# A two-layer transformer step on one core: cast order at the merge's first tile, and where the products by sevens begin in the second layer

## The reference

```
h   = rms_norm(x) * (1 + scale1) + shift1
z   = h @ w_in                       # inputs of three mixers, and three gates
g   = sigmoid(z_gate)                # (B, L, 3, 1024)
out = (g[0]*y_a + g[1]*y_b + g[2]*y_c) @ w_out
x   = x + gate1 * out
h2  = rms_norm(x) * (1 + scale2) + shift2
x   = x + gate2 * (square(relu(h2 @ w_ff1)) @ w_ff2)
```

## Time and profile before

| what | value |
|---|---|
| time, median of 3 runs (lowest to highest) | 2067.82 us (2067.37 to 2068.98) |
| the profiled execution: its own time, and its span | 2063.75 us, 2062.0 us |
| mean granted TensorE clock | 0.992 |
| busy: PE, DVE, ACT, POOL | 96%, 59%, 46%, 14% |
| the chain that ended last: PE, DVE, ACT | 82%, 11%, 3% |

### The profile page before, as it was taken

The page is one execution under the profiler, slowest core; times in us unless marked ns, Lnnn a source line. Parts: engine busy times, 40 slices in busy tenths (PEclk is TensorE's granted clock), DMA queues, the critical chain, the costliest instruction groups (busy, mean ns, idle before and its releaser), DMA issues.

```text
span 2062.0 us, 34108 instructions
## 1 busy us (share of the span) xinstructions
PE 1980.4 (96%) x13976; PEld 1810.8 (88%) x13976; DVE 1217.4 (59%) x2095; ACT 946.0 (46%) x1746; POOL 284.7 (14%) x229
## 2 busy tenths in 40 slices
PE   6999999999999999999999999999999899999997
PEld 3995688899888999999989866888999899999997
DVE  4245688756468273736553466877664764646464
ACT  5535544534366161625454355453442743535262
POOL 1000000222012130403100000003220312121210
PEclk9999999999999999999999999999999999999999
DMA  9210001343523324242432100113443121213221
GB/s 367 74 51 11 1 27 52 114 166 128 188 81 112 144 91 150 68 149 88 158 109 74 36 6 1 47 58 120 163 162 124 51 89 65 94 62 103 62 94 60
DMA packets 53035, 195.92 MB, mean 95 GB/s; under 512 B 6032, under 2 KB 8144, under 8 KB 52112
## 3 DMA queue, kind: packets, MB, share of 16 engines
q1 hardware_dynamic: 49408, 174.61, 25.2%
q0 software_dynamic: 3472, 19.14, 2.6%
HBM read 187.79 MB, written 5.93 MB: 94 GB/s over the span
## 4 chain that ended last, share of the span: by engine, by line
PE 82%; DVE 11%; ACT 3%; issue 2%; DMA 2%; SPq 0%; ACTq 0%; DVEq 0%
PE ps L742 36%; PE ps L894 23%; PE ps L809 2%; PE ps L914 2%; PE ps L1060 2%; PE ps L923 2%; DVE w_lo_parts L1687 2%; PE ps L760 2%; PE ps L1036 2%; PE ps L847 2%; PE ps L1090 2%; PE ps L1065 1%; ACT scratch L1508 1%; DVE scratch L2095 1%; DVE merged L1764 1%
## 5 line engine op out<-in xcount | busy, mean ns | idle before, releaser
L1687 DVE TENSOR_TENSOR w_lo_parts<-w_raw,w_hi_parts 128x512 fp32r<-128x512 f32 x548 | 403.9, 756 | 242.9 <-ACT w_hi_parts L1274 148.2
L1274 ACT CAST w_hi_parts<-w_raw 128x512 fp32r<-128x512 f32 x296 | 172.1, 619 | 457.5 <-PE ps L742 413.4
L742 PE MATMUL ps<-hid_hi_parts,w_hi_parts 128*128 128x320 f32 x1216 | 280.3, 312 | 2.3 <-DVE merged L2154 1.6
L742 PE MATMUL ps<-hid_lo_parts,w_hi_parts 128*128 128x320 f32 x1216 | 277.0, 309 | 0.0
L742 PE MATMUL ps<-hid_hi_parts,w_lo_parts 128*128 128x320 f32 x1216 | 276.9, 309 | 0.0
L1885 DVE SCALAR_TENSOR_TENSOR x<-ps,modulation,x 128x128 f32<-128x128 f32 (+2 forms) x216 | 81.7, 434 | 319.0 <-PE ps L742 319.0
L742 PEld LDWEIGHTS ps<-hid_hi_parts,w_hi_parts 128*128 128x128 f32 x1216 | 201.9, 188 | 25.3 <-issue 22.1
L1278 ACT CAST w_hi_parts<-w_raw 128x512 fp32r<-128x512 f32 x252 | 152.2, 621 | 137.5 <-PE ps L742 56.7
L742 PEld LDWEIGHTS ps<-hid_lo_parts,w_hi_parts 128*128 128x128 f32 x1216 | 203.3, 188 | 0.0
L742 PEld LDWEIGHTS ps<-hid_hi_parts,w_lo_parts 128*128 128x128 f32 x1216 | 203.3, 188 | 0.0
L894 PE MATMUL ps<-h_hi_parts,w_hi_parts 128*128 128x320 f32 x560 | 173.8, 310 | 0.0
(11 more groups left out here) (334 smaller groups left out, 4080.9 us busy)
## 6 DMA issues: line engine op xcount, KB each, us to landing
w_raw<-in_stream SPq DMA_DIRECT2D x312, 512.0 KB, 3.9
scratch<-in_first SPq DMA_DIRECT2D x10, 512.0 KB, 14.3
small_weights<-in_small POOLq DMA_DIRECT2D x2, 2048.0 KB, 10.5
h_scratch<-in_first SPq DMA_DIRECT2D x6, 512.0 KB, 17.3
x<-in_xT POOLq DMA_DIRECT2D x2, 1280.0 KB, 11.8
x<-in_xT POOLq DMA_DIRECT2D x8, 320.0 KB, 4.1
x_kept<-x POOLq DMA_DIRECT2D x8, 320.0 KB, 2.5
x<-x_kept POOLq DMA_DIRECT2D x8, 320.0 KB, 4.1
```

What stands on the lines that cost most here:

```text
L742: ins = mm(out[:, h, :], weight(w, s, k), a[:, k, h * HALF:(h + 1) * HALF], start=(first and n == 0), stop=(last and n == 2))
L1274: copy(place(wh, r), raw_half(s, n)).then_inc(w_hi, 1)
L1687: return tt(dst, full, hi.bitcast(F32), ALU.subtract)
```

## The change

Three edits. (1) At m = 0 of the mix, in both layers, ACT first waits for the gate product and casts the two weight halves, and only then does `first_gate(0)` (for q = 0) and the sigmoid out of PSUM; before, both sigmoids stood ahead of the casts. (2) Of the low parts at m = 0, DVE makes part 1 after b = 0, part 2 after b = 1 and part 3 after b = 2; before, parts 1 and 2 after b = 0, part 3 after b = 1. (3) In the second layer the first feed-forward block goes by sevens from tile 6 on: tiles 4 and 5 become whole products, and only the pair (6, 7) is by sevens. `first_seven(l, f)` says where it begins, and the counts of finished products (`done`) and the loops of PE, ACT and DVE follow it; ACT's two `cast_diff` stay at q = 2 and 3.

```
--- before.py
+++ after.py
@@ -118,6 +118,11 @@
 SEVEN = 7
 
 
+def first_seven(l, f):
+
+    return 0 if f > 0 else 4 if l == 0 else 6
+
+
 def by_sevens(s):
 
     i = s % PER
@@ -125,7 +130,7 @@
         m, q = divmod(i - MIX0, 3)
         return m >= 1 and q < 2
     f, q = divmod(i - FF0, 2 * KT)
-    return f >= 0 and q in (range(4, KT) if f == 0 else range(KT))
+    return f >= 0 and q in range(first_seven(s // PER, f), KT)
 
 
 def leads(s):
@@ -161,17 +166,17 @@
 PLAIN = [plain(s) for s in range(MAIN)]
 
 
-def whole_product(o):
+def whole_product(o, l):
 
     if O_MIX <= o < O_OUT:
         m, q = divmod(o - O_MIX, 5)
         return m == 0 or q >= 2
-    return o < O_FF or not by_sevens(FF0 + o - O_FF)
-
-
-def done(o):
-
-    return sum(whole_product(n) for n in range(o + 1)) + (KT if o >= O_MIX else 0)
+    return o < O_FF or not by_sevens(l * PER + FF0 + o - O_FF)
+
+
+def done(o, l=0):
+
+    return sum(whole_product(n, l) for n in range(o + 1)) + (KT if o >= O_MIX else 0)
 
 
 def blocks_until(s):
@@ -191,7 +196,7 @@
         m, q = divmod(i - MIX0, 3)
         n = done(O_MIX + 5 * m + (q if q < 2 else 3 + half))
     else:
-        n = done(O_OUT + (i - OUT0))
+        n = done(O_OUT + (i - OUT0), l)
     return l * DONE + n
 
 
@@ -1225,7 +1230,7 @@
                 last_two(0, O_OUT + OUT_TILES - 2, OUT0 + OUT_TILES - 2, hh, hl)
                 for f in range(FF_BLOCKS):
                     i, o = FF0 + 2 * KT * f, O_FF + 2 * KT * f
-                    for q in range(4 if f == 0 else 0):
+                    for q in range(first_seven(e.layer, f)):
                         if q == 0:
                             first_two(o, i, 1, True)
                         elif q > 1:
@@ -1233,9 +1238,9 @@
                             banks_read(o + q)
                             product(pair(o + q), i + q, hh, hl)
                         modulation(i + q)
-                    for q in range(4 if f == 0 else 0, KT, 2):
+                    for q in range(first_seven(e.layer, f), KT, 2):
                         n = o + q
-                        first = q == (4 if f == 0 else 0)
+                        first = q == (first_seven(e.layer, f))
                         pair_by_sevens(n, i + q, {0: n - 2, 2: n - 1} if first else {0: n - 4, 2: n - 2, 3: n - 1})
                     for q in range(KT if f < FF_BLOCKS - 1 else KT - 2):
                         tile_ready(i + KT + q)
@@ -1601,12 +1606,12 @@
 
                     if m == 0:
                         act.wait_ge(gate_sb, e.at(gate_sb, 2 * KT))
-                    if m == 0:
-                        first_gate(0)
                     for q in range(2 if m == 0 else 0):
                         act.wait_ge(mm_done, e.at(mm_done, done(o + q)))
+                        split_next(i + q)
+                        if q == 0:
+                            first_gate(0)
                         fn(halves(G[:, 1 + q, :]), pair(o + q), ACT.Sigmoid).then_inc(pair_free[(o + q) % 2], 1)
-                        split_next(i + q)
                         modulation(i + q)
                         for n in range(2 * q, 2 * q + 2):
                             cast_diff(True, n)
@@ -1640,13 +1645,14 @@
                     if f == 1:
                         act.preload_act_table_set(LN)
                     i, o = FF0 + 2 * KT * f, O_FF + 2 * KT * f
-                    for q in range(4 if f == 0 else 0):
-                        act.wait_ge(mm_done, e.at(mm_done, done(o + q)))
+                    for q in range(first_seven(e.layer, f)):
+                        act.wait_ge(mm_done, e.at(mm_done, done(o + q, e.layer)))
                         split_next(i + q)
                         fn(halves(gqk[:, q % 2, :]), pair(q), ACT.Relu).then_inc(pair_free[q % 2], 1)
-                        if q >= 2:
+                        if q in (2, 3):
                             cast_diff(False, 2 * q - 4)
                             cast_diff(False, 2 * q - 3)
+                        if q >= 2:
                             act.wait_ge(pair_free[q % 2], e.at(pair_free[q % 2], (o + q) // 2 + 1))
                             act.wait_ge(hid_ready, e.at(hid_ready, q - 1))
                             fn(hid[:, q % 2, :], gqk[:, q % 2, :], ACT.Square).then_inc(hid_sq, 1)
@@ -1658,8 +1664,8 @@
                         if q == 1:
                             full_h(1)
                         modulation(i + q)
-                    for q in range(4 if f == 0 else 0, KT, 2):
-                        pair_by_sevens(f, q, o, q == (4 if f == 0 else 0))
+                    for q in range(first_seven(e.layer, f), KT, 2):
+                        pair_by_sevens(f, q, o, q == (first_seven(e.layer, f)))
                         modulation(i + q)
                         modulation(i + q + 1)
                     hid_by_sevens(f, KT - 1, o)
@@ -1818,11 +1824,11 @@
                     if j == 0:
                         add_square(KT - 3)
                 half_sum(b, 0)
-                dve.wait_ge(mm_done, e.at(mm_done, done(o)))
+                dve.wait_ge(mm_done, e.at(mm_done, done(o, e.layer)))
                 add_half(KT - 2, o, gate, HALVES[1]).then_inc(pair_free[0], 1)
 
             def last_add(o, gate):
-                dve.wait_ge(mm_done, e.at(mm_done, done(o)))
+                dve.wait_ge(mm_done, e.at(mm_done, done(o, e.layer)))
                 add_half(KT - 1, o, gate, HALVES[1]).then_inc(pair_free[1], 1)
 
             def hat(n, p, k):
@@ -2160,7 +2166,7 @@
                         if b == 2:
                             tt(out, out, halves(tmp), ALU.add).then_inc(gate_scratch_free, 1)
                         if m == 0:
-                            for n in ((1, 2), (3,), ())[b]:
+                            for n in ((1,), (2,), (3,))[b]:
                                 low_diff(True, n)
                         if m == KT - 1:
                             for k in ((0, 1, 2), (3,), ())[b]:
@@ -2215,7 +2221,7 @@
                     for q in range(KT if f < FF_BLOCKS - 1 else KT - 2):
                         if f == 0 and q == 0:
                             dve.wait_ge(mod_read, 6 * e.layer + 6)
-                        dve.wait_ge(mm_done, e.at(mm_done, done(o + KT + q)))
+                        dve.wait_ge(mm_done, e.at(mm_done, done(o + KT + q, e.layer)))
                         add_to_x(q, q, 5).then_inc(pair_free[q % 2], 1)
                         if f == FF_BLOCKS - 1 and q >= 2:
                             add_square(q - 1)
```

6 lines of the change are left out of this document (3 added, 3 removed).

## The result

The changed kernel took 2053.32 us, median of 4 runs (2052.7 to 2056.31), against 2067.6 (2064.77 to 2068.98) for the kernel before: a ratio of 0.9933 with a 95% interval of 0.9917 to 0.9949. Timed again on another chip it took 2054.26 us (6 runs) against 2067.81 (14 runs), ratio 0.9932 (0.9918 to 0.9946). That is 14 us less, 11 to 17 by the interval.

The account below looks back on a forecast made before the run. PE, busy 96%, was taken as the bound, with DVE's queue setting its pace at the waits. Gains of 4.8 us in the mix and 4.2 in the feed-forward made 9.0 off 2067.82: 2058.8 us, range 2056.5 to 2063.4.

Parts of the forecast that it names:

- 10.5 us in 7 waits: PE's block products near the change: total time PE stood waiting for low weight halves from DVE.
- Edit 1, q = 0: Mix, both layers: casts fill ACT's wait before the sigmoids, so DVE's first low half starts 3.2 us earlier.
- Edit 1, q = 1: Mix: DVE waits 1.3 us for block 0's cast, keeping 1.9; PE loses 0.35 us per layer before b = 1.
- The same three operations in another order, so block 4's low half gains nothing: Mix, DVE: making low parts one by one brings block 4's low half no earlier, being behind all three.
- I take an unchanged toll: First layer's mix: POOL's four block sums still cost DVE some 3.5 us, as before the change.
- all four sums could block DVE: Mix: each POOL sum could cost DVE 1.1 us, 4.4 at most, making the total gain 7.2 instead of 9.0.
- Edit 3: Second layer's feed-forward: whole tiles 4 and 5 cost PE 1.76 us but remove waits, gaining 4.2 us (3.0 to 4.3).
- The same 9.0 off 2067.82: Whole kernel: the 9.0 us taken off the profiled span also comes off the runs' median, giving 2058.8 us.
- (a): Rival, mix: POOL eats DVE's head start or casts come late; only the order helps, 1.0 us; 2062.6 us, chance 0.13.
- (b): Rival, second layer's feed-forward: waits move to tile 6 and PE has 12 more matmuls; 2064.8 us, chance 0.08.
- (c): Rival, changed places: no effect, PE arrives earlier and waits for weights from memory; about 2067.5 us, chance 0.07.
- (d): Rival, mix at q = 1: sigmoid behind casts waits for a late raw tile; slower, 2072.8 us, chance 0.03.

Follow-up runs that it names:

- before_4: One traced execution of the unchanged kernel before, with clock falls in the second mix and second feed-forward; no total time given, 14 feed-forward blocks took 30.91 us.

## Why the prediction was wrong, point by point

- **PE's work and restarts:** right. 1.76 us for 12 matmuls, 0.1 for a restart.
- **"10.5 us in 7 waits" near the change:** misread in part. Three of the seven, 2.2 us, were in the first layer's feed-forward and stayed (2.0 us). The waits of 1.58 and 1.18 us that it lists as well are for other operations and not in that row. Its sums took each wait by itself and do not suffer from this.
- **Edit 1, q = 0:** right. DVE starts 3.2 us earlier against PE (362.90 + 0.41 against 366.47), the table load follows the casts without any gap.
- **Edit 1, q = 1:** right. A gap of 1.25 us on DVE (1.3 said), a wait of 0.15 us before b = 1, with its restart 0.3 (0.35 said).
- **"The same three operations in another order, so block 4's low half gains nothing", and "I take an unchanged toll":** this is the step that failed in the sum of the mix. The toll in the first layer was 1.4 us (1.1 on the low halves, 0.25 on low part 1) instead of 3.5, since the sums lay over DVE's gap and over a multiplication out of PSUM, and the new order put low part 2 behind them. Block 4's low half ended at 382.93 + 0.41 = 383.34, not 384.84, and PE was last. Mix: 3.6 + 2.9 = 6.5 us, the prediction's upper end (6.6), not 4.8. The Trainium skill (SBUF — State Buffer, "Who interferes with whom") states that a DVE operation with two inputs in SBUF contends with a GpSimd operation that reads SBUF, and one with at most one input there does not. The trace agrees: the two low halves take 1.1 us longer under the sum of 369.76, the multiplication out of PSUM keeps its 0.81 us under that of 371.69. Reading this as "all four sums could block DVE" was the misuse: what had to be asked is which DVE operation stands under each sum at its new time, and which of the two began first.
- **Edit 3:** right in kind and nearly in size, 4.5 us against 4.2. The waits did not move to tile 6.
- **"The same 9.0 off 2067.82":** this step failed for the median. It carried a difference of two undisturbed timelines over to medians. The prediction noted that its execution was 4.07 us below the median and made nothing of it; the changed kernel's profiled execution is only 0.6 below its own. In 4 of 7 executions the clock fell behind the wait at block 3 of the second mix, which was to go, and this wait then cost 1.5 us more than its length. That is 0.9 us in the mean. The rest, some 2 us of the medians, has no cause shown. With 11.0 us off the median the forecast would have been 2056.8, just inside the range: what the timelines show of the waits alone would have been held by it, and it is the part beyond them that put the time below.
- **Rivals:** (a) to (d) did not come. None of them lay on the side on which it went wrong: the range ended only 0.4 us beyond the sum of the upper ends of the steps, and no case for more gain than the waits themselves was held open. The mix alone came out at an end that it had held open (6.6).

## What to carry to other kernels

When an operation moves, lay the other engine's work at its new time over it before charging a toll; a toll ahead of a point where the engine waits anyway costs nothing. When the profiled execution is well below the median of the runs, look at several traces before carrying a difference over: the clock may fall behind the waits in question in part of the executions. Removing a wait on a nearly full TensorE can then return more than its length (1.5 us more in the mix), but nothing more where other waits follow at once (the feed-forward). Block schemes that save matmuls are worth their 12 matmuls (1.76 us) only where their operands are ready: here one pair by sevens cost 6 us of waits to save 1.76.

## What the runs showed of the hardware

- Behind a wait of 2.65 us of PE, in the second mix, the granted clock went from 2.4 to 1.2 GHz for about 3.4 us (once 6.8) in 4 of 7 executions of one program, behind the waits in the feed-forward (the first of 2.4 us) in 3 of 7, and not at all in the rest. In `before_4` 25 matmuls were done in 5 us instead of 36.
- Such a fall cost 1.5 us where PE had no wait behind it, and in 4 of 5 traces nothing where DVE's next results were waited for anyway.
- The same program took 2062.2 to 2073.9 us over 48 executions, with mean clocks from 0.993 down to 0.987, 1.2 us for each thousandth.
- Four sums of POOL cost DVE between 1.4 and 3.5 us in the first mix, by when they ran: 1.30 or 3.49 us for the same two low halves of 128x512, 1.49 or 2.59 for the same low part of 128x1280. Where the sum began second it was the sum that took longer, 1.75 or 2.36 us instead of 1.30, in the changed kernel.
- The load of an activation table came directly behind a cast, 362.96 after 361.80 + 1.14, with no time between.
